# How GpSimd leaves a stage: 21 stage ends without its drain, in a two-block transformer kernel on one core

## What is computed

```python
def first_block(x, norm1, w_in, ...):
    for layer in range(DEPTH):                       # 2
        h = rmsnorm(x, norm1[layer])
        x = x + hybrid_mixer(h, w_in[layer], ...)
        h = rmsnorm(x, norm2[layer])
        if layer % 2 == 0:
            x = x + swiglu(h, ffn_gate[j], ffn_up[j], ffn_down[j])
        else:
            x = x + moe_swiglu(h, router[j], moe_gate[j], moe_up[j], moe_down[j])
    return x

def second_block(x, mem, ...):
    for l in range(DEPTH_2):                         # 1
        h = rms_norm(x, norm_mix_g[l])
        proj = h @ w_in[l] + b_in[l]
        ...                                          # rwkv7_branch, rglru_branch, merged
        x = x + merged @ w_mix_out[l]
        x = x + cross_attention(rms_norm(x, norm_x_g[l]), rms_norm(mem, norm_mem_g[l]), ...)
        x = x + conv_ffn(rms_norm(x, norm_ffn_g[l]), ...)
    return rms_norm(x, norm_final_g)
```

## Time and profile before

| | us |
|---|---|
| median of 3 runs | 2758.16 |
| lowest and highest of them | 2752.09, 2759.08 |
| the profiled execution, its own time | 2753.02 |
| its span, first to last instruction | 2751.2 |
| mean granted clock of TensorE in it | 0.979 of full |

### The profile page before, as it was taken

How to read it: one execution, slowest core, us unless ns; L and a number is a source line. 1 busy time by engine, 2 the same in 40 slices (tenths; PEclk the granted TensorE clock), 3 DMA queues, 4 the chain that set the end, 5 groups by cost and what they waited for, 6 DMA issues and landing times. The chain is left out here.

```text
span 2751.2 us, 54709 instructions
## 1 busy us (share of the span) xinstructions
PE 2629.3 (96%) x22741; PEld 2105.2 (77%) x22741; DVE 1573.4 (57%) x1945; ACT 1187.4 (43%) x1525; POOL 310.8 (11%) x356
## 2 busy tenths in 40 slices
PE   8999999999999989999999998998899999999998
PEld 7677678888776767788888887853778787788887
DVE  6747454244484655666766666376665545454462
ACT  5544342122454443555565655345324433432232
POOL 5013000000110401011111111021410000000002
PEclk9999899999999989999999999999999999999999
DMA  4200234334220012787778776412013352234341
GB/s 138 80 9 4 62 105 114 88 92 111 70 92 20 4 53 73 272 289 278 277 280 292 278 277 219 114 31 73 6 52 118 92 147 72 75 96 109 90 111 52
DMA packets 351883, 331.12 MB, mean 120 GB/s; under 512 B 17273, under 2 KB 269525, under 8 KB 351605
## 3 DMA queue, kind: packets, MB, share of 16 engines
q1 hardware_dynamic: 348101, 317.76, 37.1%
q0 software_dynamic: 3392, 11.14, 1.1%
q10 hardware_dynamic: 240, 0.07, 0.0%
HBM read 317.41 MB, written 11.53 MB: 120 GB/s over the span
## 5 line engine op out<-in xcount | busy, mean ns | idle before, releaser
L3111 DVE TENSOR_TENSOR experts_w_lo<-experts_raw,experts_w_hi 128x2048 fp32r<-128x2048 f32 (+1 forms) x81 | 167.7, 2079 | 78.3 <-ACT experts_w_hi L3067 77.1
L3111 DVE TENSOR_TENSOR experts_w_lo<-raw_in_act,experts_w_hi 128x2048 fp32r<-128x2048 f32 (+1 forms) x81 | 167.0, 2078 | 59.0 <-ACT experts_w_hi L3067 58.7
L3067 ACT ACTIVATE experts_w_hi<-raw_in_act 128x2048 fp32r<-128x2048 f32 (+1 forms) x81 | 139.7, 1746 | 49.4 <-DMA raw_in_act<-in_moe_up 43.9
L3280 PE MATMUL experts_psum<-experts_w_hi,experts_xg_lo 128*128 128x512 f32 x384 | 155.2, 404 | 5.2 <-DVE experts_w_lo L3111 4.1
L1557 PE MATMUL proj_psum<-keep_act_hi,proj_w_lo 128*128 128x512 f32 x360 | 151.5, 421 | 5.1 <-DVE proj_w_lo L1477 5.1
L3281 PE MATMUL experts_psum<-experts_w_lo,experts_xg_hi 128*128 128x512 f32 x384 | 150.8, 393 | 0.0
L3282 PE MATMUL experts_psum<-experts_w_hi,experts_xg_hi 128*128 128x512 f32 x384 | 150.6, 392 | 0.0
L3067 ACT ACTIVATE experts_w_hi<-experts_raw 128x2048 fp32r<-128x2048 f32 (+1 forms) x81 | 140.5, 1743 | 20.9 <-DMA experts_raw<-in_moe_gate 15.0
L1559 PE MATMUL proj_psum<-keep_act_hi,proj_w_hi 128*128 128x512 f32 x360 | 141.2, 392 | 0.0
L1558 PE MATMUL proj_psum<-keep_act_lo,proj_w_hi 128*128 128x512 f32 x360 | 141.1, 392 | 0.0
L831 PE MATMUL conv_ffn_psum<-keep_act_hi,conv_ffn_w_lo 128*128 128x512 f32 x336 | 131.8, 392 | 2.0 <-DVE conv_ffn_hid_lo L880 2.0
(11 more groups left out here) (886 smaller groups left out, 6794.8 us busy)
## 6 DMA issues: line engine op xcount, KB each, us to landing
raw_in_act<-in_moe_gate SPq DMA_DIRECT2D x33, 1024.0 KB, 7.2
experts_raw<-in_moe_up SPq DMA_DIRECT2D x32, 1024.0 KB, 10.3
experts_raw<-in_moe_down SPq DMA_DIRECT2D x32, 768.0 KB, 11.7
raw_in_act<-in_moe_down SPq DMA_DIRECT2D x32, 768.0 KB, 6.7
conv_ffn_raw<-in_w_ffn_in SPq DMA_DIRECT2D x43, 512.0 KB, 5.0
experts_raw<-in_moe_gate SPq DMA_DIRECT2D x17, 1024.0 KB, 8.7
raw_in_act<-in_moe_up SPq DMA_DIRECT2D x16, 1024.0 KB, 5.2
proj_raw<-in_w_in SPq DMA_DIRECT2D x18, 768.0 KB, 4.4
```

The source lines that it names most:

```text
L3067: act.activation(w_hi[v % 2][:, s], raw[ring][:, 0:n], ACT.Copy).then_inc(rounded, 1)
L3111: dve.tensor_tensor(w_lo[v % 2][:, s], raw[ring_of(2 * v + q)][:, 0:n], w_hi[v % 2][:, s].bitcast(F32), ALU.subtract).then_inc(split, 1)
L3280: pe.matmul(out, lhs[1][:, first + k, :], w_hi[slot][:, cols], start=begin and k == 0, stop=False)
```

## The change

All 13 blocks are opened with the option `no_gpsimd_drain=True`, and one wait is added at the end of GpSimd's list in the projections. Thirteen times:

```diff
-        block = ph.enter_context(nc.Block())
+        block = ph.enter_context(nc.Block(no_gpsimd_drain=True))
```

and once, in the part of the projections that runs in both layers (L1634):

```diff
         pool.tensor_scalar(fx.q_even[HD:P, :], r.rhs_rows[HD:P, :], r.row_of_head[HD:P, 0:1], None, ALU.mult).then_inc(rows_done, 1)
+        pool.wait_ge(rows_done, ROWS + 1)
```

More of the change, by code:

```diff
@@ L1348, in turn_phase @@
         turn = turn_part(m, ph, ph.banks(), pairs, n)
-        block = ph.enter_context(m.nc.Block())
+        block = ph.enter_context(m.nc.Block(no_gpsimd_drain=True))
         @block.tensor
```

## The result

| | before | after |
|---|---|---|
| median of 20 runs each, taken together | 2759.52 | 2768.02 |
| lowest and highest | 2752.09, 2772.15 | 2753.75, 2779.48 |
| the profiled execution, its own time | 2753.02 | 2778.75 |
| its span, and mean granted clock | 2751.2, 0.979 | 2777.0, 0.969 |

The ratio is 1.0029 with an interval of 1.0016 to 1.0042: 8.5 us slower where 1.7 were forecast, and outside the range of 2751 to 2766 us. The median hides what happened: it is the middle of a gap in which no run lies. The 20 runs of after lie in two groups with nothing between 2765.4 and 2770.6: ten from 2753.75 to 2765.42, ten from 2770.61 to 2779.48. Of the 20 runs of before, two lie up there. From here on a run of 2768 us or more is called a **late run**. The question of this study became what a late run is, and why the change makes so many.

A forecast was written before the change was run, and what follows sets the result against it. PE, busy 96%, was taken to bound the kernel. Drain removal 0, added events 1.7 us and the added wait 0 took the median from 2758.16 to 2759.8 us, range 2751 to 2766, with 0.88 for within 0.3%.

The forecast's parts named there:

- GpSimd's drain is hidden: At all 21 stage ends another engine's drain ends later by 0.5 us or more, so removing GpSimd's DRAIN gains 0.
- The rival in which it is on the path: GpSimd's drains hold the meetings at every end, so 29 us would go, giving 2729 us; chance 0.04.
- The price of one event: One event more on the last-arriving engine at each of 21 ends costs 0.08 us, 1.7 us slower in sum.
- The sign of my profile test: At the end near 720 us, DVE's L889 to ACT's L271 takes 0.39 us, not 0.31.
- The added wait costs nothing: In the projections of both layers GpSimd's added wait costs 0; the meeting's events queued behind it come 107 us later.
- Each engine shifts alike, so nothing new is late: Later stages start later by the sum so far, 0.08 to 1.7 us, on all engines, with no further loss.
- the clock falls more often: Slower rival: added PE idleness at 21 places brings three longer half-clock stretches of 3.5 us, 2770 us; chance 0.06.
- The range: Forecast time of 2751 to 2766 us, from the price's bounds and the scatter of the runs before.

## Why the prediction was wrong, point by point

**GpSimd's drain is hidden: right.** No meeting became shorter, and GpSimd was last at none. The rival in which it is on the path is out.

**The price of one event: right.** I took 0.08 us an end between bounds of 0.02 and 0.31. Measured were 0.05 to 0.07 at 19 ends, mean 0.07 over all 20, and 1.4 us in sum against 1.7. The sign of my profile test came out, 0.36 us against the 0.39 that I named and the 0.31 of before. The rule of the Trainium skill that I weighed there, Perfetto Trace Analysis, section Sequencer-only Instruction (DRAIN, etc), pointed the right way: the record of the event on DVE is 21 ns, and the meeting grew by 67. Seen over the runs that are not late, the change costs 2.6 us: their medians are 2761.9 (26 runs) and 2759.2 (159 runs). The meetings account for 1.4 of it; where the rest goes is not shown.

**The added wait costs nothing: right.** The projections of both layers kept their length to 0.6 us, with the meeting's growth in it.

**"Each engine shifts alike, so nothing new is late": this step failed.** I had checked the order of the engines and not what PE's idle time does to the granted clock at the one stage that can't get it back. The rival was named, and it is what came: the clock falls more often, at one stage. Three terms of it were wrong. Its size was taken from stretches of 6.8 to 10.2 us with matmuls of 128x512, 2.3 to 3.5 us each, so that I needed three of them to reach 2770. In the scan the fall lasts for the whole stage, and 576 matmuls of 64x64 in a chain with DVE go from 221 to 224 ns up to 315 to 318 ns: one single fall costs 12.1 us (the medians of late and other runs of the change, 2774.9 and 2761.9, lie 13.0 apart). Its chance of 0.06 rested on "0.08 us on top of an idle time of PE of 1.6 us and more around an end is very little", which speaks of one end, while 45% of executions are late against 7%. And 1.6 us was misread for the end that counts: most ends of the profile before have about 1.6 us or more, but at the one ahead of the scan PE idles for 1.07 us, and four others have 0.7 to 1.2. What turned that little into so many late runs is the open question above. A reader of the profile before could have asked at which stage one fall would cost most. The scan stands behind a meeting at which PE idles for 1.1 us and behind two waits for code, and two runs of 20 of the kernel before are late.

**The range** took the scatter of three runs, 2752 to 2759, for that of the kernel. Twelve of 171 runs of before are late, and three runs show none of them four times in five. With that group in it the range would have reached 2772 at least. Whether the median lay in it was then a matter of the session: the same kernel gave 2768.02, 2768.16 and 2762.25 us in its three sets, and the last lies inside. The step above is wrong for all three.

## What to carry to other kernels

A median over two groups of executions moves when their shares move. Look at the list of runs first, and at the granted clock of each, before looking for the microseconds in a stage. A limit in microseconds that tells the groups apart in one kernel can miss them in the next. Find the stage in which a clock that fell stays down to the end (in all seven profiles with the fall, here), and price one fall there by the whole stage. Throwaway work on PE up to the meeting ahead of it took the changed kernel from 6 late runs of 12 to none of 12 in one session; in the kernel before they are too rare to tell. And an option that removes an instruction from the engine that is never last buys nothing, while what it adds on the last one is paid at every end.

## What the runs showed of the hardware

- At a meeting of five engines, one event more on each engine that arrives lengthens it by 49 to 74 ns at 19 of 20 ends, with a record of 17 to 21 ns for the event on SP, ACT and DVE.
- A clock that fell at the scan's start stayed at half for 44.4 us, with PE busy 93% of the time or more in 64x64 matmuls of 316 ns. It came back only in the next stage, behind matmuls of 128x512.
- The same program waits for code 0.6 us at one place in one execution and 0.9 us in another.
- Fifty-five turns of the identity taken out of a wait at the start of the experts' stage made that stage 50 us longer in the profiled run; its five runs took 2808 to 2828 us.
